# The first products of two feed-forwards, taken with 512 moving columns instead of 256

## The chip, the cores and the metric

One core of one Trainium2 chip. The metric is the device time of one execution of the whole program in microseconds (us), lower is better. Times are medians of several executions.

## What is computed

A transformer block (recurrent unit beside latent attention, cross attention to a memory, feed-forward) and a second one (dilated and differential attention, feed-forward, gated linear attention, eight experts), for 256 tokens of width 1024, all in 32-bit floats. The change touches the first half of the two feed-forwards alone:

```python
# first block: D_FF = 2816, w_up is 1024 x 5632
gu = rms_norm(x, ffn_norm) @ w_up
gu = depthwise_conv(gu, ffn_conv_w, ffn_conv_b, 1, 1)     # 3 taps over the tokens, per column
g, u = gu[..., :D_FF], gu[..., D_FF:]
x = x + (jax.nn.silu(g) * u) @ w_down

# second block: the same without the convolution
h = rms_norm_2(x, ffn_norm_2)
x = x + (jax.nn.silu(h @ w_gate) * (h @ w_up)) @ w_down
```

## The kernel before

**Numbers in two parts.** TensorE multiplies 32-bit numbers in a form (fp32r) that holds fewer bits. So each operand is kept as a rounded part and the rest, and a product is the sum of three: rounded x rounded, rounded x rest, rest x rounded. `wh` and `wl` are the two parts of the weights, `hTh` and `hTl` those of the 256 normalised tokens (features on the partitions, tokens along the row, 8 tiles `k` of 128 features).

**Weights as a stream.** All weights lie in HBM as 458 units of 128 x 2048 numbers (1 MB). SyncE loads them one after another into 7 buffers `raw`, each as soon as VectorE is through with the unit 7 before it. ScalarE rounds each unit into one of 3 buffers `wh` (`hi_to`, L1444 to L1451, instruction L1450), as soon as the product that used the buffer before is done. VectorE subtracts and gets the rest into `wl` (`lo_to`, L2203 to L2209, instruction L2207). `hi_to(m)` and `lo_to(m)` stand in the programs of the two engines where the author put them, and each engine does its instructions strictly in order.

**A feed-forward.** 22 rounds `f`, one unit each: 128 columns of the gate and 128 of the up projection (`i` = 0 and 1). In `gated` (L819) TensorE makes both with `feature_major` (L549), through `split_product` (L419): for each of 8 `k` a matmul of the rounded weights with 256 columns of rounded tokens (L424) and one with 256 columns of rests (L428), both adding into the same 256 columns of PSUM, then 8 matmuls of the rests of the weights with the rounded tokens (L435). So a round has 48 matmuls of 256 moving columns. The rounds go through PSUM banks 0 to 3, gate and up side by side in one bank; a round waits for the read of the one four before (`gated_read`).

In the first feed-forward ScalarE then forms the middle tap and bias out of PSUM (L1750, two instructions of 256 columns) and rounds the unit three rounds ahead (L1450); VectorE forms the rest of that unit (L2207), adds the two outer taps out of PSUM (L2635, four instructions of 255 columns, with a wait on its own result after the second), and for the round before it does sigmoid x gate (L2644) and x up (L2645), and for the round before that the rest of the hidden value (L2623). ScalarE does the sigmoid (L1757) and the rounding of the hidden value (L1761). In the second feed-forward there is no convolution: VectorE multiplies bank `f % 4` with the row of token scales (L2860, 512 columns) into `gu2`, and then come sigmoid (L1904), L2865, L2866, L2207, L2623.

`project_out` (L533) then multiplies the 22 hidden tiles with the second weights: 11 units, 24 matmuls of 512 columns each, into banks 4 to 7.

Of the kernel before, what the change touches and what calls it, by code (L numbers as in the profile page):

```python
# [26 lines left out]
P = 128  # L27
# [80 lines left out]
def build(nc, units_d, consts_d, cols_d, rows_d, lru_w_d, x_d, mem_d, pos_d, out_d):  # L108
# [8 lines left out]
    hT_at = nc.sbuf_base  # L117
    hTh = sb("hTh", [KD, S], F32R)
    hTl = sb("hTl", [KD, S], F32R)
    xn = sb("xn", [TT, D])  # L120
# [43 lines left out]
    def row(name, n):  # L164
# [18 lines left out]
        "gu": dict(ffn=FT, ffn2=FT), "in_copied": dict(lru=8, mem=6), "in_read": dict(attn=12, hgrn=14),  # L183
        "gated": dict(lru=1, hgrn=2), "product": dict(lru=2, ffn=FT, ffn2=FT),
        "in": dict(lru=8, mem=8, attn=16, hgrn=24), "gated_sigmoid": dict(ffn=FT, ffn2=FT), "gated_read": dict(ffn=FT, ffn2=FT),
# [65 lines left out]
    cv = [[xn[:, b // 2, 512 * (b % 2) + 256 * i:512 * (b % 2) + 256 * (i + 1)] for i in range(2)] for b in range(4)]  # L251
    sg = [area(12288 + 256 * b, S) for b in range(4)]
    gu2 = [xn[:, b // 2, 512 * (b % 2):512 * (b % 2 + 1)].rearrange("p (i s) -> p i s", i=2) for b in range(4)]

# [149 lines left out]
    def _(pe):  # L404
# [144 lines left out]
        def feature_major(out, w, c):  # L549
# [3 lines left out]
                                 ready=tile_ready, weights="stationary")  # L553

        def token_major(name, n0, srch, srcl, banks, width=HALF):

            for half in range(2):
                w = by_k(unit(n0 + half), KD // 2, width)
                for t in range(TT):
                    ts = slice(t * P, (t + 1) * P)  # L560
                    ks = [4 * half + k for k in range(4)]
                    ins = split_product(ps[:, banks[t], 0:width],
                                        [(srch[:, k, ts], srcl[:, k, ts], w[0][:, k - 4 * half, :], w[1][:, k - 4 * half, :])
                                         for k in ks], first=(half == 0), last=(half == 1),
                                        ready=lambda j: tile_ready(4 * half + j))
                    if half == 1 or t == 1:
                        counted(ins, name)
                release(n0 + half, name)
# [249 lines left out]

        def gated(stage, n0):  # L819
            for f in range(FT):  # L820
                w = by_k(unit(n0 + f), KD, S)
                if f >= 4:
                    pe.wait_ge(*reached(stage + "_gated_read", f - 3))
                for i in range(2):
                    ins = feature_major(ps[:, f % 4, i * S:(i + 1) * S], w, i)
                counted(ins, stage + "_gu")
                release(n0 + f, stage + "_gu")
                if f == 0 and stage == "ffn2":
                    pe.wait_ge(*reached("scale_diag", 1))
                    counted(accumulate(ps[:, 4, 0:S], [(ones, scale_diag.rearrange("p t c -> p (t c)"))]), "scale_ps")  # L830

        norm("ffn_norm")
        gated("ffn", UNITS_AT["w_up"])
        project_out("ffn_x_change", UNITS_AT["w_down"], FT, hidh, hidl, lambda k: pe.wait_ge(*reached("ffn_hid", k + 1)))

# [216 lines left out]
        norm("ffn_norm_2")  # L1052
        gated("ffn2", UNITS_AT["ffn_gate_up"])
        project_out("ffn2_x_change", UNITS_AT["ffn_w_down"], FT, hidh, hidl,
# [385 lines left out]
    def _(act):  # L1440
# [302 lines left out]
        for f in range(FT + 2):  # L1743
            if f < FT:
                act.wait_ge(*reached("ffn_gu", f + 1))
                if f >= 4:
                    act.wait_ge(*reached("ffn_product", f - 3))
                for i in range(2):
                    c = f + i * FT
                    ins = A(cv[f % 4][i], ps[:, f % 4, i * S:(i + 1) * S], ACT.Identity,  # L1750
                            scale=col("ffn_conv_w", 2 * FT + c), bias=col("ffn_conv_b", c))
                ins.then_inc(sem("ffn_centre"), 1)
                hi_to(UNITS_AT["w_up"] + f + 4)
            if 1 <= f <= FT:
# [144 lines left out]
        scales(1)  # L1899
        for f in range(FT + 2):  # L1900
            hi_to(UNITS_AT["ffn_gate_up"] + f + 4)
            if f < FT:
# [284 lines left out]
    def _(dve):  # L2187
# [438 lines left out]
        for f in range(FT + 2):  # L2626
            if f < FT:
                dve.wait_ge(*reached("ffn_centre", f + 1))
                lo_to(UNITS_AT["w_up"] + f + 4)
                for tap in range(2):  # L2630
                    for i in range(2):
                        w = col("ffn_conv_w", tap * 2 * 2 * FT + f + i * FT)
                        y, src = cv[f % 4][i], ps[:, f % 4, i * S:(i + 1) * S]
                        a, b = (slice(1, S), slice(0, S - 1)) if tap == 0 else (slice(0, S - 1), slice(1, S))
# [222 lines left out]
        for f in range(FT + 2):  # L2857
            if f < FT:
                dve.wait_ge(*reached("ffn2_gu", f + 1))
                V.tensor_tensor(gu2[f % 4], ps[:, f % 4, :].rearrange("p (i s) -> p i s", i=2), both,  # L2860
                                ALU.mult).then_inc(sem("ffn2_gated_read"), 1)
            if 1 <= f <= FT:
# [508 lines left out]
```

## Time and profile before

| | |
|---|---|
| median of 3 executions | 1872.81 us (1871.18 to 1873.44) |
| the profiled execution, its own time | 1872.04 us |
| its span, first to last instruction | 1870.2 us |
| TensorE busy | 1824.6 us, 98% |
| VectorE busy | 1477.8 us, 79% |
| ScalarE busy | 1232.8 us, 66% |
| mean granted TensorE clock | 0.994 |
| moved from and to HBM | 492 MB, mean 263 GB/s |

The profile calls TensorE PE (its weight loads PEld), VectorE DVE, ScalarE ACT. Busy time of TensorE is no measure of its pace, since its matmuls overlap: one of 256 columns is shown as 284 ns long while they start every 120 ns. The pace is read from the distance of starts. In a row of the view in order of time the first number is the start, the second the duration, both in us; where a row merges several instructions (x4), the duration is that of all.

### The profile page before, as it was taken

The page shows a single profiled execution, that of the slowest core. Times are in us where ns is not written, and L with a number is a line of the kernel's source. Part 1 is how long each engine was busy: PE and PEld are TensorE (multiplying, and loading weights), DVE is VectorE, ACT ScalarE, POOL GpSimd, SP SyncE. Part 2 cuts the span into 40 slices and gives each one's busy share as a digit, 9 for nine tenths or more (in the row PEclk, how much of TensorE's full clock was granted, in tenths as well). Part 3 has the DMA queues.
Part 4 walks back from the last instruction along what each step waited for, and adds up shares of the span by engine and source line. Part 5 has one row for each costly group of instructions (what it writes and reads, how often), then busy time and mean ns, then how long its engine had stood idle before and what let it go on. Part 6 is the DMA issues. An engine that isn't in the chain of part 4 may idle for free.

```text
span 1870.2 us, 25929 instructions
## 1 busy us (share of the span) xinstructions
PE 1824.6 (98%) x9976; PEld 1558.8 (83%) x9976; DVE 1477.8 (79%) x1502; ACT 1232.8 (66%) x1292; POOL 25.5 (1%) x27
## 2 busy tenths in 40 slices
PE   9989999999899999999999999999999999999998
PEld 7867899887789998987788888888888888888886
DVE  7975688657667765675988988889889899898886
ACT  6966556455654434663777777777777777777775
POOL 0000000000000000000000000000000000000000
PEclk9999999999999999999999999999999999999999
DMA  9422445543235554534699999999999999999994
GB/s 356 158 86 90 158 180 181 202 174 117 73 115 189 187 184 144 185 125 146 229 381 358 391 373 358 375 364 391 376 343 378 374 391 367 341 391 372 379 378 162
DMA packets 69091, 491.97 MB, mean 263 GB/s; under 512 B 7792, under 2 KB 8176, under 8 KB 10096
## 3 DMA queue, kind: packets, MB, share of 16 engines
q1 hardware_dynamic: 67248, 484.33, 68.0%
q0 software_dynamic: 1728, 6.03, 1.6%
q8 instruction: 81, 1.33, 0.3%
q14 instruction: 34, 0.28, 0.0%
HBM read 485.09 MB, written 5.24 MB: 262 GB/s over the span
## 4 chain that ended last, share of the span: by engine, by line
PE 86%; DVE 7%; ACT 5%; issue 2%; POOL 0%; DVEq 0%; ACTq 0%; POOLq 0%
PE ps L424 26%; PE ps L433 20%; PE ps L426 20%; PE ps L435 5%; PE ps L428 5%; DVE wl L2207 2%; PE ps L1370 1%; ACT wh L1450 1%; PE ps L444 1%; PE ps L1271 1%; PE ps L584 1%; DVE hTl L2265 1%; ACT hTh L1488 1%; PE ps L854 1%; PE ps L855 1%
## 5 line engine op out<-in xcount | busy, mean ns | idle before, releaser
L3163 DVE TENSOR_TENSOR wl<-raw,wh 128x2048 fp32r<-128x2048 f32 x334 | 761.2, 2291 | 88.1 <-ACT wh L2089 87.4
L2089 ACT ACTIVATE wh<-raw 128x2048 fp32r<-128x2048 f32 x333 | 637.9, 1918 | 182.5 <-PE ps L433 182.5
L424 PE MATMUL ps<-wh,hTh 128*128 128x512 f32 (+2 forms) x1128 | 443.0, 394 | 5.5 <-DVE hTl L2538 1.5
L426 PE MATMUL ps<-wh,hTl 128*128 128x512 f32 (+2 forms) x1128 | 434.7, 386 | 0.0
L2207 DVE TENSOR_TENSOR wl<-raw,wh 128x2048 fp32r<-128x2048 f32 x124 | 283.6, 2290 | 123.8 <-ACT wh L1450 123.4
L1450 ACT ACTIVATE wh<-raw 128x2048 fp32r<-128x2048 f32 x125 | 238.6, 1914 | 138.0 <-PE ps L433 70.2
L433 PE MATMUL ps<-wl,hTh 128*128 128x512 f32 (+2 forms) x1128 | 300.9, 386 | 0.0
L424 PE MATMUL ps<-wh,work_r 128*128 128x512 f32 x648 | 254.8, 393 | 0.0
L424 PEld LDWEIGHTS ps<-wh,hTh 128*128 128x128 f32 x1128 | 212.0, 188 | 48.8 <-issue 4.2
L426 PE MATMUL ps<-wh,work_r 128*128 128x512 f32 x648 | 252.5, 390 | 0.0
L426 PEld LDWEIGHTS ps<-wh,hTl 128*128 128x128 f32 x1128 | 212.2, 188 | 40.1
L433 PEld LDWEIGHTS ps<-wl,hTh 128*128 128x128 f32 x1128 | 209.8, 188 | 42.9
L424 PE MATMUL ps<-hTh,wh 128*128 128x256 f32 x896 | 223.5, 286 | 4.3 <-DVE hTl L2265 4.0
L428 PE MATMUL ps<-hTl,wh 128*128 128x256 f32 x896 | 221.4, 284 | 0.0
L433 PE MATMUL ps<-wl,work_r 128*128 128x512 f32 x648 | 200.3, 390 | 0.5 <-DVE wl L3163 0.5
L424 PEld LDWEIGHTS ps<-hTh,wh 128*128 128x128 f32 x896 | 171.7, 192 | 7.5 <-issue 5.0
L428 PEld LDWEIGHTS ps<-hTl,wh 128*128 128x128 f32 x896 | 171.8, 192 | 0.1
L433 PEld LDWEIGHTS ps<-wl,work_r 128*128 128x128 f32 x648 | 121.2, 188 | 28.1 <-DVE wl L3163 2.8
L424 PEld LDWEIGHTS ps<-wh,work_r 128*128 128x128 f32 x648 | 121.7, 188 | 25.7 <-issue 1.0
L426 PEld LDWEIGHTS ps<-wh,work_r 128*128 128x128 f32 x648 | 121.7, 188 | 24.5
L435 PE MATMUL ps<-hTh,wl 128*128 128x256 f32 x896 | 126.3, 284 | 0.0
L435 PEld LDWEIGHTS ps<-hTh,wl 128*128 128x128 f32 x896 | 116.1, 192 | 0.0
(442 smaller groups left out, 1548.9 us busy)
## 6 DMA issues: line engine op xcount, KB each, us to landing
raw<-in_units SPq DMA_DIRECT2D x458, 1024.0 KB, 6.8
x<-in_x SPq DMA_DIRECT2D x2, 512.0 KB, 5.9
work<-in_lru_w SPq DMA_DIRECT2D x1, 1024.0 KB, 16.0
xn<-in_mem SPq DMA_DIRECT2D x1, 1024.0 KB, 14.2
out<-x POOLq DMA_DIRECT2D x2, 512.0 KB, 6.4
consts<-in_consts POOLq DMA_DIRECT2D x1, 768.0 KB, 4.5
consts<-in_consts SPq DMA_DIRECT2D x1, 356.0 KB, 12.5
cols<-in_cols SPq DMA_DIRECT2D x1, 202.0 KB, 2.6
```

What stands on the lines that cost most here:

```text
L424: nc.tensor.matmul(out, sh, mh, start=(first and j == 0), stop=False)
L426: nc.tensor.matmul(out, sl, mh, start=False, stop=False)
L428: nc.tensor.matmul(out, sh, ml, start=False, stop=False)
L433: ins = nc.tensor.matmul(out, sh, ml, start=False, stop=done)
L435: ins = nc.tensor.matmul(out, sl, mh, start=False, stop=done)
L444: ins = nc.tensor.matmul(out, l, r, start=(first and j == 0), stop=(last and j == len(pairs) - 1))
L584: nc.tensor.matmul(ps[:, 7, :], junk[:, 0:P], junk[:, 0:HALF], start=True, stop=True)
L854: nc.tensor.matmul(out, hTh[:, k, ts], hi[:, o], start=first, stop=False, skip_group_check=u == 2)
L1450: A(wh[:, n % SPLIT, :], raw[:, n % RAW, :], ACT.Copy).then_inc(sem("hi_made"), 1)
L2089: A(wh[:, n % SPLIT, :], raw[:, n % RAW, :], ACT.Copy).then_inc(sem("hi_made"), 1)
L2207: V.tensor_tensor(wl[:, n % SPLIT, :], raw[:, n % RAW, :], wh[:, n % SPLIT, :].bitcast(F32), ALU.subtract).then_inc(sem("lo_made"), 1)
L3163: V.tensor_tensor(wl[:, n % SPLIT, :], raw[:, n % RAW, :], wh[:, n % SPLIT, :].bitcast(F32), ALU.subtract).then_inc(sem("lo_made"), 1)
```

## The change

`hTh` and `hTl` become the two halves of one buffer `hT_both` at the same place. In the new `halves_beside` one matmul per `k` takes the rounded tokens and the rests, 512 moving columns, against the rounded weights, and writes 512 columns of PSUM: the first 256 hold rounded x rounded, the others rounded x rest. The 8 matmuls of the weights' rests add into the first 256 as before. Gate and up now have a bank each, so a round fills two banks and every second round uses the same ones. What the matmuls no longer add has to be added afterwards: ScalarE copies the first halves (2 x 256 columns) out of PSUM into SBUF, VectorE adds the second halves (2 x 256 columns, read from PSUM). In the first feed-forward middle tap and outer taps then read that sum from SBUF; in the second, the sum is multiplied with the scales in SBUF. TensorE waits for the sum of the round two before (`summed`) in place of the read of the one four before. In the first feed-forward ScalarE rounds the next weights ahead of the middle tap instead of behind it, and VectorE waits for `ffn_centre` behind the weights' rest instead of ahead of it.

```diff
-    hTh = sb("hTh", [KD, S], F32R)
-    hTl = sb("hTl", [KD, S], F32R)
+    hT_both = sb("hT_both", [2, KD, S], F32R)
+    hTh, hTl = hT_both[:, 0, :, :], hT_both[:, 1, :, :]
...
+    gu = [area(11264 + 512 * b, 2, S) for b in range(2)]
...
+        def halves_beside(out, w, c):
+
+            cs = slice(c * P, (c + 1) * P)
+            for k in range(KD):
+                tile_ready(k)
+                nc.tensor.matmul(out, w[0][:, k, cs], hT_both[:, :, k, :], start=(k == 0), stop=False)
+            rest_made()
+            for k in range(KD):
+                ins = nc.tensor.matmul(out[:, 0:S], w[1][:, k, cs], hTh[:, k, :], start=False, stop=(k == KD - 1))
+            return ins
...
-        def gated(stage, n0):
+        def gated_beside(stage, n0):
             for f in range(FT):
                 w = by_k(unit(n0 + f), KD, S)
-                if f >= 4:
-                    pe.wait_ge(*reached(stage + "_gated_read", f - 3))
+                if f >= 2:
+                    pe.wait_ge(*reached(stage + "_summed", f - 1))
                 for i in range(2):
-                    ins = feature_major(ps[:, f % 4, i * S:(i + 1) * S], w, i)
+                    ins = halves_beside(ps[:, 2 * (f % 2) + i, :], w, i)
...
@@ ScalarE, first feed-forward
                 act.wait_ge(*reached("ffn_gu", f + 1))
+                b = 2 * (f % 2)
+                A(gu[f % 2], ps[:, b:b + 2, 0:S], ACT.Copy).then_inc(sem("ffn_first"), 1)
+                hi_to(UNITS_AT["w_up"] + f + 4)
                 if f >= 4:
                     act.wait_ge(*reached("ffn_product", f - 3))
+                act.wait_ge(*reached("ffn_summed", f + 1))
                 for i in range(2):
                     c = f + i * FT
-                    ins = A(cv[f % 4][i], ps[:, f % 4, i * S:(i + 1) * S], ACT.Identity,
+                    ins = A(cv[f % 4][i], gu[f % 2][:, i, :], ACT.Identity,
                             scale=col("ffn_conv_w", 2 * FT + c), bias=col("ffn_conv_b", c))
                 ins.then_inc(sem("ffn_centre"), 1)
-                hi_to(UNITS_AT["w_up"] + f + 4)
@@ ScalarE, second feed-forward
+            if f < FT:
+                b = 2 * (f % 2)
+                act.wait_ge(*reached("ffn2_gu", f + 1))
+                A(gu2[f % 4], ps[:, b:b + 2, 0:S], ACT.Copy).then_inc(sem("ffn2_first"), 1)
             hi_to(UNITS_AT["ffn_gate_up"] + f + 4)
@@ VectorE, first feed-forward
+                b = 2 * (f % 2)
+                dve.wait_ge(*reached("ffn_first", f + 1))
+                V.tensor_tensor(gu[f % 2], ps[:, b:b + 2, S:2 * S], gu[f % 2], ALU.add).then_inc(sem("ffn_summed"), 1)
+                lo_to(UNITS_AT["w_up"] + f + 4)
+                dve.wait_ge(*reached("ffn_summed", f + 1))
                 dve.wait_ge(*reached("ffn_centre", f + 1))
-                lo_to(UNITS_AT["w_up"] + f + 4)
...
-                        y, src = cv[f % 4][i], ps[:, f % 4, i * S:(i + 1) * S]
+                        y, src = cv[f % 4][i], gu[f % 2][:, i, :]
@@ VectorE, second feed-forward
                 dve.wait_ge(*reached("ffn2_gu", f + 1))
-                V.tensor_tensor(gu2[f % 4], ps[:, f % 4, :].rearrange("p (i s) -> p i s", i=2), both,
-                                ALU.mult).then_inc(sem("ffn2_gated_read"), 1)
+                b = 2 * (f % 2)
+                dve.wait_ge(*reached("ffn2_first", f + 1))
+                V.tensor_tensor(gu2[f % 4], ps[:, b:b + 2, S:2 * S], gu2[f % 4], ALU.add).then_inc(sem("ffn2_summed"), 1)
+                dve.wait_ge(*reached("ffn2_summed", f + 1))
+                V.tensor_tensor(gu2[f % 4], gu2[f % 4], both, ALU.mult).then_inc(sem("ffn2_gated_read"), 1)
```

In the order of the instructions this is a round of the first feed-forward on VectorE, before (L2207 makes the weights' rest, L2635 are the outer taps, L2644 and L2645 the products, L2623 the hidden value's rest; in brackets what an instruction waits for):

```order
L2207 TENSOR_TENSOR wl<-raw,wh 128x2048 [waits hi_made,ffn_centre]
L2635 SCALAR_TENSOR_TENSOR xn<-ps,cols,xn 128x255 x2
L2635 SCALAR_TENSOR_TENSOR xn<-ps,cols,xn 128x255 [waits vector_step]
L2635 SCALAR_TENSOR_TENSOR xn<-ps,cols,xn 128x255
L2644 TENSOR_TENSOR work<-work,xn 128x256 [waits gated_read,gated_sigmoid]
L2645 TENSOR_TENSOR work<-work,xn 128x256 [waits vector_step]
L2623 TENSOR_TENSOR work_r<-work,work_r 128x256 [waits hid_hi]
```

and now, with the new line numbers (L2649 is the sum of the halves, L2226 the weights' rest, L2658 the outer taps):

```order
L2649 TENSOR_TENSOR work<-ps,work 128x512 [waits first]
L2226 TENSOR_TENSOR wl<-raw,wh 128x2048 [waits hi_made]
L2658 SCALAR_TENSOR_TENSOR xn<-work,cols,xn 128x255 [waits ffn_centre,summed]
L2658 SCALAR_TENSOR_TENSOR xn<-work,cols,xn 128x255
L2658 SCALAR_TENSOR_TENSOR xn<-work,cols,xn 128x255 [waits vector_step]
L2658 SCALAR_TENSOR_TENSOR xn<-work,cols,xn 128x255
L2667 TENSOR_TENSOR work<-work,xn 128x256 [waits gated_read,gated_sigmoid]
L2668 TENSOR_TENSOR work<-work,xn 128x256 [waits vector_step]
L2642 TENSOR_TENSOR work_r<-work,work_r 128x256 [waits hid_hi]
```

The sum stands ahead of the weights' rest, which no longer waits for ScalarE's middle tap. On TensorE a round of the first feed-forward is now this (L561 with both kinds of columns, L564 the weights' rests; there are two such pairs of lines to a round):

```order
L561 MATMUL ps<-hT_both,wh 128x512 [waits summed,hi_made]
L561 MATMUL ps<-hT_both,wh 128x512 x7
L564 MATMUL ps<-hT_both,wl 128x256 [waits lo_made]
L564 MATMUL ps<-hT_both,wl 128x256 x7
L561 MATMUL ps<-hT_both,wh 128x512 x8
L564 MATMUL ps<-hT_both,wl 128x256 [waits lo_made]
L564 MATMUL ps<-hT_both,wl 128x256 x7
```

That is 16 matmuls of 512 columns and 16 of 256 in place of 48 of 256.

## Rows read from the trace of the kernel before

**Rows 1.** The page: busy time by engine, and the DMA engines in 40 slices.
```profile
PE 1824.6 (98%) x9976; PEld 1558.8 (83%) x9976; DVE 1477.8 (79%) x1502; ACT 1232.8 (66%) x1292; POOL 25.5 (1%) x27
...
DMA  9422445543235554534699999999999999999994
```

**Rows 2.** By stretch: us; busy (x) of PE, PEld, DVE, ACT, POOL; PEclk, DMA share, GB/s.
```profile
203.30:208.40 5.10, 5.09 (x24) 5.10 (x25) 5.10 (x8) 2.94 (x5) 0.00 (x0) 0.52 0.00 0
208.40:332.30 123.90, 123.90 (x1035) 123.90 (x1034) 103.68 (x160) 72.59 (x103) 0.00 (x0) 1.00 0.53 187
547.00:675.00 128.00, 127.89 (x1058) 127.26 (x1059) 91.55 (x113) 59.69 (x74) 0.00 (x0) 1.00 0.50 182
1000.00:1860.00 860.00, 859.46 (x3941) 711.73 (x3941) 758.82 (x458) 640.11 (x447) 19.31 (x15) 1.00 0.95 365
```

**Rows 3.** TensorE in order of time, first feed-forward, 24 matmuls (half a round) apart.
```profile
263.12 0.28 PE L424 MATMUL ps<-hTh,wh 128*128 128x256 f32 x1
...
265.04 1.12 PE L435 MATMUL ps<-hTh,wl 128*128 128x256 f32 x8
266.00 0.28 PE L424 MATMUL ps<-hTh,wh 128*128 128x256 f32 x1
```

**Rows 4.** TensorE in order of time, 512-column matmuls of a product going out.
```profile
349.95 0.39 PE L424 MATMUL ps<-wh,work_r 128*128 128x512 f32 x1
...
352.67 0.39 PE L424 MATMUL ps<-wh,work_r 128*128 128x512 f32 x1
```

**Rows 5.** TensorE in order of time, attention input: 512 columns behind 256.
```profile
411.08 1.12 PE L859 MATMUL ps<-wl,hTh 128*128 128x256 f32 x8
412.04 0.40 PE L854 MATMUL ps<-wh,hTh 128*128 128x512 f32 x1
...
413.88 1.07 PE L859 MATMUL ps<-wl,hTh 128*128 128x512 f32 x4
```

**Rows 6.** VectorE in order of time, first feed-forward, one round and the next start.
```profile
260.49 2.29 DVE L2207 TENSOR_TENSOR wl<-raw,wh 128x2048 fp32r<-128x2048 f32 x1 [0.65 <-ACT wh L1450]
262.70 1.78 DVE L2635 SCALAR_TENSOR_TENSOR xn<-ps,cols,xn 128x255 f32<-128x255 f32 x4
264.39 0.42 DVE L2644 TENSOR_TENSOR work<-work,xn 128x256 f32<-128x256 f32 x1
264.84 0.42 DVE L2645 TENSOR_TENSOR work<-work,xn 128x256 f32<-128x256 f32 x1
265.19 0.42 DVE L2623 TENSOR_TENSOR work_r<-work,work_r 128x256 fp32r<-128x256 f32 x1
266.25 2.29 DVE L2207 TENSOR_TENSOR wl<-raw,wh 128x2048 fp32r<-128x2048 f32 x1 [0.64 <-ACT wh L1450]
```

**Rows 7.** ScalarE in order of time, the same round of the first feed-forward.
```profile
257.56 1.02 ACT L1750 ACTIVATE xn<-ps,cols 128x256 f32<-128x256 f32 x2 [2.33 <-PE ps L435]
258.47 1.91 ACT L1450 ACTIVATE wh<-raw 128x2048 fp32r<-128x2048 f32 x1
260.28 0.41 ACT L1757 ACTIVATE work<-xn 128x256 f32<-128x256 f32 x1
260.58 0.41 ACT L1761 ACTIVATE work_r<-work 128x256 fp32r<-128x256 f32 x1
```

**Rows 8.** VectorE, second feed-forward, in order of time.
```profile
565.83 0.69 DVE L2860 TENSOR_TENSOR xn<-ps,junk 128x512 f32<-128x512 f32 x1 [1.46 <-PE ps L435]
566.44 0.42 DVE L2865 TENSOR_TENSOR work<-work,xn 128x256 f32<-128x256 f32 x1
...
567.84 2.29 DVE L2207 TENSOR_TENSOR wl<-raw,wh 128x2048 fp32r<-128x2048 f32 x1 [0.53 <-ACT wh L1450]
```

**Rows 9.** Groups of instructions by line and form: those nearest to the new ones.
```profile
L1933 ACT ACTIVATE work<-ps 128x512 f32<-128x512 f32 x4 | 2.3, 585 | 0.0
L2394 DVE SCALAR_TENSOR_TENSOR work<-work,cols 128x256 f32<-128x256 f32 x24 | 10.0, 480 | 0.3
L2573 DVE TENSOR_TENSOR work<-work 128x512 f32<-128x512 f32 x2 | 1.4, 692 | 0.4 <-ACT work L1689 0.4
```

More of the change, by code:

```diff
@@ L183, in build @@
         "gu": dict(ffn=FT, ffn2=FT), "in_copied": dict(lru=8, mem=6), "in_read": dict(attn=12, hgrn=14),
-        "gated": dict(lru=1, hgrn=2), "product": dict(lru=2, ffn=FT, ffn2=FT),
+        "first": dict(ffn=FT, ffn2=FT), "summed": dict(ffn=FT, ffn2=FT), "gated": dict(lru=1, hgrn=2), "product": dict(lru=2, ffn=FT, ffn2=FT),
         "in": dict(lru=8, mem=8, attn=16, hgrn=24), "gated_sigmoid": dict(ffn=FT, ffn2=FT), "gated_read": dict(ffn=FT, ffn2=FT),
@@ L832, in _ @@
         norm("ffn_norm")
-        gated("ffn", UNITS_AT["w_up"])
+        gated_beside("ffn", UNITS_AT["w_up"])
         project_out("ffn_x_change", UNITS_AT["w_down"], FT, hidh, hidl, lambda k: pe.wait_ge(*reached("ffn_hid", k + 1)))
@@ L1052, in _ @@
         norm("ffn_norm_2")
-        gated("ffn2", UNITS_AT["ffn_gate_up"])
+        gated_beside("ffn2", UNITS_AT["ffn_gate_up"])
         project_out("ffn2_x_change", UNITS_AT["ffn_w_down"], FT, hidh, hidl,
```

## Prediction

> **What bounds the kernel now.** I read the page first. TensorE is busy 98% of the span, VectorE 79%, ScalarE 66% [rows 1]. A busy TensorE says little about its pace, so I went to the stretches. The first feed-forward's 22 rounds run from 203.3 to 332.3 us, the second's from 547 to 675 us; in both TensorE is covered from end to end, and the DMA engines are about half busy (0.53 and 0.50) [rows 2]. So neither stage waits for weights, and whatever shortens TensorE's work there shortens the kernel, as long as the other engines keep up. The DMA line climbs to 9 tenths only in the second half [rows 1], in the experts (0.95 over 860 us) [rows 2]. That does not swallow a gain: SyncE's loads are released by VectorE's use of older units, not by the clock, so if a feed-forward ends earlier, every later load moves with it.
>
> The pace of TensorE is read from starts. In the feed-forward 24 matmuls of 256 columns take 263.12 to 266.00 = 2.88 us, 120 ns each [rows 3]; a round is 48 of them, 5.76 us. A product of 512 columns starts every 226.7 ns (12 in 2.72 us) [rows 4]. At the granted clock of 1.00, the level of 2.4 GHz [rows 2], the columns alone are 106.7 and 213.3 ns, so both sizes carry the same 13.3 ns on top. That is what the change goes for: the columns stay the same (48 x 256 = 16 x 512 + 16 x 256), the instructions fall from 48 to 32.
>
> **TensorE's new round.** By the two paces alone a half round is 8 x 226.7 + 8 x 120 = 2.77 us instead of 2.88. But the program has a place with just the new pattern: in the attention's input a run of 8 matmuls of 512 columns stands right behind 256-column ones, and it takes 412.04 to 413.88 = 1.84 us, 230 ns each, 0.03 more than 8 x 226.7 [rows 5]. The 8 ahead of it take 0.96 us (411.08 to 412.04), the 120 ns of always. I take this row, since the new kernel goes from 256 to 512 columns in every half round: 1.84 + 0.96 = 2.80 us, 0.08 less than now, 5.60 us a round. Of 2 x 44 = 88 half rounds two are left out: the first of the first stage runs at a granted clock of 0.52, nearly all at the 1.2 GHz level [rows 2], where fewer instructions showed me no saving, and the first of the second waits for its inputs tile by tile. 86 x 0.08 = **6.9 us saved**. The upper end is 0.107 (226.7 ns from the first matmul on), 9.2 us. The lower end is nothing: no row has a moving operand in two pieces 8 KB apart, and were the 13.3 ns paid per 256 columns of a piece, 512 would cost 240. I stay near the upper end because a contiguous 512 is the nearest row.
>
> The Trainium skill ("TensorE: Matmul & The Clock Gate", section Back-to-back issue gap) gives N / 2.4 + 2.5 ns as the gap of isolated warm matmuls, that is 2.5 ns an instruction. By that rule the 86 x 8 = 688 removed instructions would be worth 1.7 us. The rows above show 13.3, so here trace and rule differ.
>
> **VectorE in the first feed-forward.** This is the tight place. A round by starts: rest of the weights 2.21 (260.49 to 262.70), four outer taps 1.69, the two products 0.45 and 0.35, the hidden rest another 0.35 taken from the like-sized one before it: 5.05 us, then 0.64 us idle until ScalarE's `wh` [rows 6]. Added is a sum of 512 columns; the nearest row is the 512-column product with one operand in PSUM, 0.69 us long, with the next instruction 0.61 us behind it [rows 8]. New round: 5.66 us, against 5.60 of TensorE. At the other end, if the next one waits for its full length and a semaphore (0.75), 5.80; if it overlapped wholly, 5.05. That the taps now read SBUF changes nothing: 480 ns for a 256-column one from SBUF [rows 9], four of 255 from PSUM in 1.78 us [rows 6].
>
> VectorE being 0.06 slower does not stall TensorE at once, because there is slack. A fresh round would go: ScalarE's copy ends 0.65 us after TensorE's round (585 ns [rows 9]), the sum ends at 1.3, but `wh` is ready only at 2.6 (1.91 us behind the copy [rows 7]); then 5.05 more, so the next sum starts at 7.65, that is 2.05 us after the end of TensorE's next round. From there on `wh` is ready in time and the lag grows by 0.06 a round. TensorE needs the sum of round f when it begins round f+2, 5.60 us after the end of round f: the lag may be 5.60 - 0.75 = 4.85. Slack 2.8 us, growth over 18 rounds 1.1: **no stall, 0 us**. At 5.80 the growth is 3.6, a stall of 0.8. Behind the 22nd round VectorE drains its lag under the outgoing product, whose first three units have their parts made by then; the fourth is needed 16.3 us (3 x 24 x 226.7 ns) after the stage ends, its rest 0.9 later, and lag, sum, weights, taps, two rounds' products, hidden rounding and the two parts of that unit add up to about 14.4 (3.2 + 0.6 + 2.2 + 1.7 + 2.0 + 0.5 + 1.9 + 2.3).
>
> **ScalarE, first stage.** Round by starts: middle tap 0.91, rounding of weights 1.81, sigmoid 0.30, hidden rounding 0.41 at most [rows 7], plus the copy 0.59: 4.0 of 5.60 us. It now waits for the sum too, but everything it owes VectorE comes at most 2 us after that sum, while VectorE has 2.21 us of weights to do: 0 us.
>
> **Second stage.** VectorE idles 1.46 + 0.53 = 2.0 us a round [rows 8]. Added: the sum in its full length, since its own result is awaited, 0.75; the product with the scales stays at 0.69 out of SBUF (692 ns for such a one) [rows 9]. 1.25 us of idle become what is left, less 0.16 of shorter round. TensorE's new wait, for the sum of two rounds ago, is met about 1.4 us after that round: 0 us. ScalarE has room.
>
> **Sum.** -6.9 us. The profiled execution's own time is 1872.04 us, 1.8 above its span; it becomes 1865.1. The median of the runs is 0.8 above that execution, so the forecast for the median is 1872.8 - 6.9 = **1865.9 us**, -0.37%. Runs differ by about 0.1%, and 0.2% (3.7 us) is about what a measurement of this kernel can tell from no change; faster means below 1869.1.
>
> **Rivals.**
> (a) *The full saving.* Runs of 512 start at 226.7 ns at once: -9.2, 1863.6 us. For it: most 512-column rows. Against: the one run behind 256 columns.
> (b) *VectorE binds the first stage mildly.* The stall is 18 x (round - 5.60) - 2.8 us. For a round of 5.90, 2.6 us, 1868.5; of 6.14, 6.9 us, 1872.8. For it: only 0.06 us is missing already, and semaphore waits have been added. Against: the parts of the round are read from starts, and the sum has a row close to it.
> (c) *Instructions are not what costs.* The two-piece operand takes 240 ns: no gain, 1872.8 us. By the skill's 2.5 ns it would be 1871.1. For it: no row shows two pieces. Against: the same 13.3 ns at both sizes.
> (d) *Slower: VectorE's round above 6.14 us*, from where the loss in the first stage exceeds the whole saving. Its place would be the wait for `wh` (1.3 us in a fresh round, above) coming back in every round instead of once: because ScalarE's copy and rounding now stand behind its own wait for the sum of the round before. The round would be 5.66 + 1.3 = 6.96, the stall 18 x 1.36 - 2.8 = 21.7, the time 1887.6 us. From the sum's end ScalarE needs 0.91 + 0.30 + 0.41 + 0.59 + 1.91, with waits 4.4 us, and VectorE comes to that point 5.66 us later; it decides if that path grows by over 1.2 us. Nothing in the rows does that.
>
> **How the numbers follow.** Forecast (1864.8 to 1867.0) 0.63, (a) 0.14, (b) 0.10, (c) 0.06, (d) 0.07. Faster: 0.63 + 0.14 + half of (b) = 0.82; same: the other half and (c) = 0.11; slower 0.07. The range 1863.0 to 1868.9 holds the forecast, (a) and the milder half of (b), 0.82.
>
> **What would show it.** Right: starts of the 512-column matmuls in the stages 227 to 233 ns apart, rounds of 5.60 us (5.55 for (a)) in both stages, VectorE without idle time from the third round on in the first stage, and TensorE without a wait for `summed`; the experts as long as before, only earlier. Wrong: 240 ns starts (c); TensorE waiting for VectorE's sum late in the first stage (b) or in every round (d); the second stage gaining no 3.4 us while the first does, or something behind the stages growing by what they saved.

## The result, and the profile after

| | before | changed |
|---|---|---|
| median of 5 executions each | 1871.51 us (1871.18 to 1873.44) | 1862.87 us (1861.71 to 1864.01) |
| ratio | | 0.9948, 95% interval 0.9937 to 0.9959 |
| profiled execution, own time | 1872.04 | 1861.83 |
| its span | 1870.2 | 1859.7 |
| instructions of TensorE (matmuls) | 9976 | 9272 |

The change made the kernel 8.6 us faster (by the interval of the ratio 7.7 to 11.8). The forecast was 6.9 us and 1865.9 us, and the measured time lies 0.1 us below the lower end of the range. The page of the changed kernel, busy time by engine and the DMA engines in 40 slices:

```profile
PE 1815.2 (98%) x9272; PEld 1518.8 (82%) x9272; DVE 1502.6 (81%) x1546; ACT 1260.7 (68%) x1336; POOL 25.5 (1%) x27
...
DMA  9422455543235554444699999999999999999994
```

TensorE has 704 matmuls fewer, VectorE and ScalarE have 44 instructions more each, and the picture is otherwise that of [rows 1]. By stretch, with the stages' new bounds (us; busy time and count of PE, PEld, DVE, ACT, POOL; granted clock, DMA share, GB/s):

```profile
202.49:327.20 124.71, 124.71 (x705) 109.18 (x705) 119.45 (x186) 89.42 (x129) 0.00 (x0) 0.99 0.51 186
390.26:536.69 146.43, 138.68 (x777) 113.20 (x777) 98.08 (x180) 88.23 (x167) 0.00 (x0) 0.98 0.32 113
539.87:664.18 124.31, 124.21 (x707) 108.38 (x707) 104.17 (x134) 72.05 (x95) 0.00 (x0) 1.00 0.52 187
664.18:1859.50 1195.32, 1180.04 (x5762) 981.29 (x5760) 993.12 (x727) 835.38 (x649) 24.06 (x21) 1.00 0.84 320
```

The first stage took 128.9 us before (203.3 to 332.2) and 124.7 now, the second 128.1 and 124.3: 4.2 and 3.8 us less. All that lies behind the second stage takes 1195.5 us (the last row stops 0.2 us short of the end), against 1195.2 from the same point before: what the stages save reaches the end. TensorE in order of time, first stage:

```profile
257.37 2.00 PE L561 MATMUL ps<-hT_both,wh 128*128 128x512 f32 x8
259.21 1.11 PE L564 MATMUL ps<-hT_both,wl 128*128 128x256 f32 x8
260.16 2.00 PE L561 MATMUL ps<-hT_both,wh 128*128 128x512 f32 x8
262.00 1.12 PE L564 MATMUL ps<-hT_both,wl 128*128 128x256 f32 x8
262.95 2.00 PE L561 MATMUL ps<-hT_both,wh 128*128 128x512 f32 x8
```

Eight matmuls of 512 columns take 1.84 us from start to start (257.37 to 259.21), just as in [rows 5], the eight of 256 behind them 0.95. A half round is 2.79 us, in place of 2.88 [rows 3]. VectorE, one round of the first stage:

```profile
256.91 0.68 DVE L2649 TENSOR_TENSOR work<-ps,work 128x512 f32<-128x512 f32 x1
257.51 2.28 DVE L2226 TENSOR_TENSOR wl<-raw,wh 128x2048 fp32r<-128x2048 f32 x1
259.71 1.79 DVE L2658 SCALAR_TENSOR_TENSOR xn<-work,cols,xn 128x255 f32<-128x255 f32 x4
261.41 0.42 DVE L2667 TENSOR_TENSOR work<-work,xn 128x256 f32<-128x256 f32 x1
261.87 0.43 DVE L2668 TENSOR_TENSOR work<-work,xn 128x256 f32<-128x256 f32 x1
262.21 0.42 DVE L2642 TENSOR_TENSOR work_r<-work,work_r 128x256 fp32r<-128x256 f32 x1
262.54 0.68 DVE L2649 TENSOR_TENSOR work<-ps,work 128x512 f32<-128x512 f32 x1
```

Where [rows 6] had 0.64 us of idle there is none: the round is 262.54 - 256.91 = 5.63 us, and it is longer than TensorE's 5.59. Who waited for whom in the first stage (us in total, times, longest):

```profile
ACT work L1759 <- PE ps L564: 23.2, 22, 4.7
ACT xn L1766 <- DVE work L2649: 13.4, 19, 1.2
DVE wl L2226 <- ACT wh L1462: 3.7, 4, 1.4
```

ScalarE waits for VectorE's sum in 19 rounds, up to 1.2 us; VectorE waited for `wh` in its first rounds only (1.1, 1.0 and 0.2 us; the fourth wait of the row, 1.4 us, lies behind the stage); no wait of TensorE for the sum is in the list, in this stage or in the second.

**Where the rest of the difference lies.** The two profiled spans differ by 10.5 us, 8.0 of it in the stages. The kernel starts its first product 0.9 us earlier, and the attention between the stages took 148.5 us before, 2.1 more than now, with the same instructions:

```profile
395.31:543.83 148.52, 139.89 (x776) 114.89 (x777) 98.35 (x180) 88.15 (x167) 0.00 (x0) 0.97 0.31 111
```

That row is of the kernel before; its granted clock is 0.97, that of the changed kernel there 0.98. The experiments show whether this belongs to the change.

### The profile page after: what moved, and what is told of

The parts are those of the page before. It is cut to its first block, busy times and chain, and to the rows that moved or that the text cites. A ratio compares the mean times of both kernels' runs of the same rounds, so it can differ in the third digit from the quotient of the medians.

```text
span 1859.7 us, 24634 instructions
## 1 busy us (share of the span) xinstructions
PE 1815.2 (98%) x9272; PEld 1518.8 (82%) x9272; DVE 1502.6 (81%) x1546; ACT 1260.7 (68%) x1336; POOL 25.5 (1%) x27
## 3 DMA queue, kind: packets, MB, share of 16 engines
q8 instruction: 76, 1.25, 0.3%
## 4 chain that ended last, share of the span: by engine, by line
PE 85%; DVE 7%; ACT 5%; issue 2%; POOL 0%; DVEq 0%; ACTq 0%; POOLq 0%
PE ps L425 21%; PE ps L434 20%; PE ps L427 20%; PE ps L561 9%; PE ps L564 5%; DVE wl L2226 2%; ACT wh L1462 1%; PE ps L1382 1%; PE ps L445 1%; PE ps L1283 1%; PE ps L436 1%; PE ps L429 1%; PE ps L596 1%; ACT hT_both L1500 1%; DVE hT_both L2284 1%
## 5 line engine op out<-in xcount | busy, mean ns | idle before, releaser
L425 PE MATMUL ps<-wh,hT_both 128*128 128x512 f32 (+2 forms) x1128 | 443.0, 394 | 5.5 <-DVE hT_both L2557 1.5
L427 PE MATMUL ps<-wh,hT_both 128*128 128x512 f32 (+2 forms) x1128 | 434.7, 386 | 0.0
L2226 DVE TENSOR_TENSOR wl<-raw,wh 128x2048 fp32r<-128x2048 f32 x124 | 283.2, 2288 | 94.0 <-ACT wh L1462 93.7
L434 PE MATMUL ps<-wl,hT_both 128*128 128x512 f32 (+2 forms) x1128 | 300.9, 386 | 0.0
L425 PEld LDWEIGHTS ps<-wh,hT_both 128*128 128x128 f32 x1128 | 212.0, 188 | 48.8 <-issue 4.2
L427 PEld LDWEIGHTS ps<-wh,hT_both 128*128 128x128 f32 x1128 | 212.2, 188 | 40.2
L434 PEld LDWEIGHTS ps<-wl,hT_both 128*128 128x128 f32 x1128 | 209.9, 188 | 42.9
L561 PE MATMUL ps<-hT_both,wh 128*128 128x512 f32 x704 | 179.0, 395 | 2.7 <-DVE hT_both L2284 2.5
L561 PEld LDWEIGHTS ps<-hT_both,wh 128*128 128x128 f32 x704 | 127.0, 190 | 27.5 <-issue 3.0
L564 PEld LDWEIGHTS ps<-hT_both,wl 128*128 128x128 f32 x704 | 96.4, 191 | 7.0
L564 PE MATMUL ps<-hT_both,wl 128*128 128x256 f32 x704 | 98.4, 283 | 0.0
L2118 ACT ACTIVATE work<-ps 128x512 f32<-128x512 f32 x56 | 33.5, 599 | 40.7 <-PE ps L434 40.7
L425 PE MATMUL ps<-hT_both,wh 128*128 128x256 f32 x192 | 48.6, 290 | 2.1 <-DVE hT_both L2284 2.0
```

Of the source, the lines that this page charges most:

```text
L425: nc.tensor.matmul(out, sh, mh, start=(first and j == 0), stop=False)
L427: nc.tensor.matmul(out, sl, mh, start=False, stop=False)
L434: ins = nc.tensor.matmul(out, sh, ml, start=False, stop=done)
L561: nc.tensor.matmul(out, w[0][:, k, cs], hT_both[:, :, k, :], start=(k == 0), stop=False)
L564: ins = nc.tensor.matmul(out[:, 0:S], w[1][:, k, cs], hTh[:, k, :], start=False, stop=(k == KD - 1))
L2118: A(esg, ps[:, 2 * (c % 2), :], ACT.Silu).then_inc(sem("gate_silu"), 1)
```

## The experiments

Two theories of what pays: the number of TensorE's instructions (each removed one is worth a fixed time), or what came with it (banks, order on ScalarE and VectorE). And two on VectorE: its round of 5.63 us binds, or slack covers it. Stage times below run from the first matmul of a stage to the first of the outgoing product.

| kernel | first stage | between | second stage | behind | span |
|---|---|---|---|---|---|
| before | 128.9 | 214.8 | 128.1 | 1195.2 | 1870.2 |
| changed | 124.7 | 212.7 | 124.3 | 1195.5 | 1859.7 |
| first stage only | 124.6 | 212.7 | 128.1 | 1196.9 | 1864.8 |
| second stage only | 128.7 | 212.6 | 124.3 | 1197.0 | 1865.9 |
| two of 256 for each 512 | 128.9 | 213.2 | 128.1 | 1196.7 | 1870.3 |
| 16 of 512, then 16 of 256 | 124.9 | 213.2 | 123.9 | 1195.5 | 1860.7 |
| one piece of 512 | 125.4 | 213.2 | 124.6 | 1196.5 | 1863.0 |
| one VectorE instruction more | 128.5 | 213.9 | 124.3 | 1195.5 | 1864.5 |
| two more | 134.6 | 215.6 | 125.7 | 1195.4 | 1873.7 |
| old order on ScalarE and VectorE | 183.8 | 221.0 | 125.6 | 1195.4 | 1929.1 |
| changed, once more | 125.0 | 213.3 | 124.3 | 1196.9 | 1862.7 |
| 16 of 512, then 16 of 256, once more | 124.5 | 213.2 | 123.9 | 1195.3 | 1858.5 |

**One stage at a time.** In `e1_first_only` the second stage has the old `gated`, copy and sum removed there:

```diff
-        gated_beside("ffn2", UNITS_AT["ffn_gate_up"])
+        gated("ffn2", UNITS_AT["ffn_gate_up"])
```

> Only the first feed-forward is changed, the second is as before. Theory A (each matmul removed is worth a fixed part of some 11 ns, 0.087 us a half round): 3.8 us in the rounds of the first stage, plus about 0.5 us in its first half round if the clock rises as early as in the changed kernel; so 3.8 to 4.5 us faster than before, half rounds of 2.79 us in the first stage and 2.88 in the second. Theory B (VectorE, at 5.64 us a round, takes part of it back in the first stage): TensorE waits for the sum of the halves, gain under 3 us. Theory C (part of the 8.6 us is the clock in other stages, not the change): the profile shows other stages differing by more than 1 us where the granted clock differs.

Measured: 1867.06 against 1872.79 us, ratio 0.9972 (0.9963 to 0.9982). `e2_second_only` has the old code in the first stage:

```diff
-        gated_beside("ffn", UNITS_AT["w_up"])
+        gated("ffn", UNITS_AT["w_up"])
```

> Only the second feed-forward is changed. Theory A: 43 half rounds x 0.087 = 3.7 us faster than before. Together with the first stage alone this should give 7.5 to 8.2 us; what the changed kernel gained beyond that would be the clock in other stages or the measurement (theory C).

Measured: 1868.11 against 1872.79 us, ratio 0.9975 (0.9966 to 0.9984). By medians the gains are 5.7 and 4.7 us, together 10.4, both above what was expected (3.8 to 4.5, and 3.7) and together above the 8.6 of the whole change. By stage times they are 4.3 and 3.7, together 8.0, as expected. The changed stage has the same length whether or not the other is changed (124.6 and 124.7; 124.3 and 124.3), so by the stages the two gains add, and VectorE takes nothing back in the first (theory B falls). The stretches between and behind differ by up to 2 us among kernels that are the same there. Behind the second stage there is a pattern. Seven of the twelve profiles have 1195.2 to 1195.5 us there, five have 1196.5 to 1197.0. In these five, and in no other, the granted clock from 725 to 750 us is 0.93 in place of 1.00. The changed kernel stands on both sides. The first row is its second profile, the other its first one:

```profile
731.00:741.00 10.00, 9.37 (x61) 8.95 (x62) 8.35 (x14) 7.03 (x14) 0.00 (x0) 0.83 0.38 141
731.00:741.00 10.00, 9.91 (x81) 9.51 (x80) 8.50 (x10) 7.15 (x12) 0.00 (x0) 1.00 0.56 204
```

So theory C holds for that stretch: its 1 to 2 us go with the clock, whichever kernel it is.

**Is it the number of instructions?** Everything of the change stays, only the 512 columns are written as twice 256:

```diff
-                nc.tensor.matmul(out, w[0][:, k, cs], hT_both[:, :, k, :], start=(k == 0), stop=False)
+                nc.tensor.matmul(out[:, 0:S], w[0][:, k, cs], hTh[:, k, :], start=(k == 0), stop=False, skip_group_check=True)
+                nc.tensor.matmul(out[:, S:2 * S], w[0][:, k, cs], hTl[:, k, :], start=False, stop=(k == KD - 1), skip_group_check=True)
             rest_made()
             for k in range(KD):
-                ins = nc.tensor.matmul(out[:, 0:S], w[1][:, k, cs], hTh[:, k, :], start=False, stop=(k == KD - 1))
+                ins = nc.tensor.matmul(out[:, 0:S], w[1][:, k, cs], hTh[:, k, :], start=False, stop=(k == KD - 1), skip_group_check=True)
```

> Everything as in the changed kernel (banks, copy, sum, order on ScalarE and VectorE), but each 512-column matmul is written as two of 256 into the two halves of the bank, 48 matmuls a round again. Theory A: half rounds back at 2.88 us, time within 1.5 us of before. Theory D (the gain comes from the new order on the other engines or the banks, not from the number of instructions): it stays near the changed kernel, 7 to 9 us faster than before. VectorE has 0.12 us idle a round in the first stage, so no stall is expected.

Measured: 1873.38 us, ratio 1.0002 (0.9993 to 1.0011). TensorE, the starts of two half rounds:

```profile
257.83 0.28 PE L562 MATMUL ps<-hT_both,wh 128*128 128x256 f32 x1
...
259.39 1.12 PE L565 MATMUL ps<-hT_both,wl 128*128 128x256 f32 x8
260.36 0.28 PE L561 MATMUL ps<-hT_both,wh 128*128 128x256 f32 x1
...
262.27 1.12 PE L565 MATMUL ps<-hT_both,wl 128*128 128x256 f32 x8
263.24 0.28 PE L561 MATMUL ps<-hT_both,wh 128*128 128x256 f32 x1
```

260.36 to 263.24 is 2.88 us again, and both stages are back at 128.9 and 128.1. So the gain in the stages comes from the 704 joined pairs; banks, copy, sum and order together are worth nothing there and cost nothing (theory D falls). Copy and sum, 88 instructions, are fully hidden. One thing this run does not separate: each matmul has a weight load of its own, and with 9976 matmuls in place of 9272 it has as many more weight loads, although the two halves use the same weights. Whether the saved time belongs to the matmul or to its weight load is not shown; below, "instruction" means the two together.

**What a change from 256 to 512 columns costs.** All 16 matmuls of 512 columns of a round first, then all 16 of 256:

```diff
+            for c in range(2):
+                cs = slice(c * P, (c + 1) * P)
+                for k in range(KD):
+                    tile_ready(k)
+                    nc.tensor.matmul(outs[c], w[0][:, k, cs], hT_both[:, :, k, :], start=(k == 0), stop=False)
             rest_made()
...
+            for c in range(2):
+                cs = slice(c * P, (c + 1) * P)
+                for k in range(KD):
+                    ins = nc.tensor.matmul(outs[c][:, 0:S], w[1][:, k, cs], hTh[:, k, :], start=False, stop=(k == KD - 1))
```

> In each round all 16 matmuls of 512 columns come first, then all 16 of 256: one change from 256 to 512 a round in place of two. Theory A with a price for each such change (0.03 us, 8 matmuls of 512 in 1.84 instead of 1.81 us): a round of 5.56 instead of 5.59 us, 44 x 0.03 = 1.3 us faster than the changed kernel, if VectorE's 5.64 us a round in the first stage lets it; there the growth of its lag is 0.08 a round, 1.5 us over 18 rounds, inside the slack of 2.8, so still no stall. Rival (every run of 512 columns is slower by 3 ns a matmul in this stage, wherever it begins): a round stays at 5.59, same time as the changed kernel.

Measured: 1862.53 us, 0.3 us below the changed kernel's median where 1.3 was expected, ratio 0.9941 (0.9928 to 0.9955). TensorE, second stage:

```profile
603.95 3.82 PE L562 MATMUL ps<-hT_both,wh 128*128 128x512 f32 x16
607.60 2.08 PE L567 MATMUL ps<-hT_both,wl 128*128 128x256 f32 x16
609.52 3.82 PE L562 MATMUL ps<-hT_both,wh 128*128 128x512 f32 x16
```

Sixteen of 512 take 3.65 us, that is 0.03 more than 16 x 226.7 ns = 3.627, where two runs of eight take 3.68. A round is 5.57 us, and the second stage 0.4 us shorter (22 x 0.02). The starts in the trace say where the extra time sits. Averaged over the first stage behind its first round, the distances behind the first five matmuls of a run of 512 are 233, 236, 228, 232 and 231 ns, and from the sixth on 226.7, in the changed kernel's runs of 8 and in these of 16 alike: 0.028 us a run. Part of it comes back: the first matmul of 256 behind a run of 512 has the next one 113 ns behind it and the second 119, where the others have 120. So a pair of changes, 256 to 512 and back, costs 0.020 us, and a run of 16 saves one such pair a round.

**One piece or two.** The moving 512 columns are one run of 2 KB; this sums rounded tokens of two tiles, and leaves the rests of the tokens out:

```diff
-                tile_ready(k)
-                nc.tensor.matmul(out, w[0][:, k, cs], hT_both[:, :, k, :], start=(k == 0), stop=False)
+                tile_ready(min(k + 1, KD - 1))
+                j = min(k, KD - 2)
+                nc.tensor.matmul(out, w[0][:, k, cs], hTh[:, j:j + 2, :].rearrange("p k s -> p (k s)"), start=(k == 0), stop=False)
```

> The 512 moving columns lie in one piece of 2 KB (rounded tokens of tiles k and k+1) in place of two pieces 8 KB apart; the rests of the tokens are left out and other products are summed, so only the time counts. Theory A: a run of 8 still takes 1.84 us behind 256-column matmuls, time as the changed kernel within 1 us. Rival (the two pieces cost the extra 3 ns a matmul): runs of 8 in 1.81 us, 88 x 0.03 = 2.6 us faster than the changed kernel.

Measured: 1865.22 us, ratio 0.9964 (0.9953 to 0.9976). TensorE, first stage:

```profile
256.02 2.00 PE L562 MATMUL ps<-hT_both,wh 128*128 128x512 f32 x8
257.86 1.12 PE L565 MATMUL ps<-hT_both,wl 128*128 128x256 f32 x8
258.81 2.00 PE L562 MATMUL ps<-hT_both,wh 128*128 128x512 f32 x8
```

1.84 and 2.79 us, to the hundredth those of the changed kernel: the gap of 8 KB costs nothing. Its time is 2.3 us above the changed kernel's 1862.87 (1.25 above the 1863.97 of its second series), more than the 1 us I expected. Its stages are 0.7 and 0.3 us longer: in the first half round of each it waits for one tile more than the changed kernel. Behind the stages it is one of the five profiles with the lower clock at 725 to 750 us, 1.0 us longer than the changed kernel's first.

**How near VectorE is to the limit.** One and two more instructions in each round of the first stage:

```diff
                 ins.then_inc(sem("ffn_gated_read"), 1)
+                V.tensor_tensor(junk[:, 0:256], consts[:, 0:S], consts[:, 0:S], ALU.mult)
```

> One more VectorE instruction of 256 columns (SBUF, result unused, 0.34 us from start to start) in every round of the first feed-forward, behind the outer taps. Theory of the slack: round of VectorE 5.64 + 0.34 = 5.98 us against 5.59 of TensorE; its lag grows by 0.39 a round, reaches the allowed 4.85 us after about 7 rounds, and TensorE then waits 18 x 0.39 - 2.8 = 4.3 us in all: about 1867.5 us. Rival (no slack: every round is the longer of the two, 22 x 0.39 = 8.6 us, some 1871.5). Rival (VectorE is not near any limit): as the changed kernel.

> Two such instructions. Round of VectorE 6.32, growth 0.73 a round, stall 18 x 0.73 - 2.8 = 10.4 us, so about 1873.5 us, the gain of the change gone and a little more. Against one extra instruction the step should be 18 x 0.34 = 6.1 us, since the slack is spent already.

Measured: 1868.75 us, ratio 0.9985 (0.9975 to 0.9995), and 1875.75 us, ratio 1.0018 (1.0009 to 1.0028). The medians lie 1.25 and 2.25 us above the expected 1867.5 and 1873.5. The first stage, which the theory is about, takes 3.8 and 9.9 us more than in the changed kernel, expected 4.3 and 10.4, and the step between them is 6.1, as expected; the rest lies outside that stage or in the scatter of the executions. The slack is real: without it one instruction would have cost 8.6 us. Its size came out a little larger than reckoned: with one more instruction VectorE's lag grows by 0.38 us a round and stops growing at 5.1 us, in the eleventh round, not at 4.85 after about seven. With two, TensorE waits in each of the last 14 rounds (two of them; the idle time before, and what ended it, in brackets):

```profile
293.57 2.08 PE L561 MATMUL ps<-hT_both,wh 128*128 128x512 f32 x8 [0.47 <-DVE work L2649]
...
299.88 2.06 PE L561 MATMUL ps<-hT_both,wh 128*128 128x512 f32 x8 [0.48 <-DVE work L2649]
```

299.88 - 293.57 = 6.31 us is VectorE's round.

**The order on ScalarE and VectorE.** As the changed kernel, but with the two engines' old order:

```diff
@@ ScalarE
-                hi_to(UNITS_AT["w_up"] + f + 4)
                 if f >= 4:
                     act.wait_ge(*reached("ffn_product", f - 3))
...
                 ins.then_inc(sem("ffn_centre"), 1)
+                hi_to(UNITS_AT["w_up"] + f + 4)
@@ VectorE
-                lo_to(UNITS_AT["w_up"] + f + 4)
                 dve.wait_ge(*reached("ffn_summed", f + 1))
                 dve.wait_ge(*reached("ffn_centre", f + 1))
+                lo_to(UNITS_AT["w_up"] + f + 4)
```

> As the changed kernel, but in the first feed-forward ScalarE forms the middle tap ahead of the rounding of the next weights, and VectorE waits for the middle tap ahead of the weights' rest, as before the change. Then sum, middle tap and rounding stand in a row in each round: VectorE idles from the end of its sum for 0.92 + 1.85 + 0.1 = 2.9 us, its round is 0.75 + 2.9 + 5.0 = 8.6 us, less what it could do meanwhile (nothing, its order is fixed). Stall 18 x 3.0 - 2.8 = 51 us: about 1914 us. This is rival (d) of the prediction made true. If instead the order does not matter, the time is the changed kernel's.

Measured: 1930.15 us, ratio 1.0307 (1.0290 to 1.0325). VectorE's round, then ScalarE's, then TensorE:

```profile
254.05 0.68 DVE L2649 TENSOR_TENSOR work<-ps,work 128x512 f32<-128x512 f32 x1
257.85 2.29 DVE L2226 TENSOR_TENSOR wl<-raw,wh 128x2048 fp32r<-128x2048 f32 x1 [3.12 <-ACT wh L1462]
...
262.89 0.68 DVE L2649 TENSOR_TENSOR work<-ps,work 128x512 f32<-128x512 f32 x1
```

```profile
254.83 1.09 ACT L1765 ACTIVATE xn<-work,cols 128x256 f32<-128x256 f32 x2 [4.85 <-DVE work L2649]
255.83 1.89 ACT L1462 ACTIVATE wh<-raw 128x2048 fp32r<-128x2048 f32 x1
```

```profile
254.88 3.65 PE L561 MATMUL ps<-hT_both,wh 128*128 128x512 f32 x8 [3.02 <-DVE work L2649]
258.36 1.11 PE L564 MATMUL ps<-hT_both,wl 128*128 128x256 f32 x8
```

VectorE idles 3.1 us in every round, which from the fifth on is 262.89 - 254.05 = 8.84 us long, and TensorE waits for the sum. Expected 8.6 and 1914 us; it is 16 us worse. The first stage is 59.1 us longer than in the changed kernel, 8 more than the 51 expected, of which the longer round explains 18 x 0.24 = 4 us. The other 8 us lie between the stages (221.0 us against 212.7), where the program is the same. The clock goes with this: between the stages its mean is 0.96 against 0.98, and in the first stage (203.2 to 387.0 us) it is 0.90 against 0.99. The run of eight behind the wait of 3.02 us takes 3.48 us in place of 1.84, near the 3.41 us of 8 x 512 columns at the 1.2 GHz level:

```profile
203.20:387.00 183.80, 143.37 (x704) 121.71 (x705) 118.58 (x185) 83.94 (x124) 0.00 (x0) 0.90 0.35 123
```

So the two lines that the change moves, and that look like a detail in the diff, are worth 67 us between the two kernels, 59 of them in the stage itself.

**Changed kernel and runs of 16 side by side.** Neither kernel has a new edit.

> The changed kernel once more, on the same chip and against the same runs of before as the next one. The stages alone give 7.5 us (86 half rounds x 0.087) and 0.5 us more where the first half round meets the higher clock; with the single stages' 5.7 and 4.7 us as measured it would be up to 10.4. Theory of the clock (a time moves by a microsecond or two with where the low-clock windows fall outside the changed stages): the gain lies between 8 and 10 us and the runs with a higher mean clock are the shorter ones.

> The order with 16 matmuls of 512 and then 16 of 256 a round once more, beside the changed kernel. Rounds of 5.57 in place of 5.59 us in both stages: 44 x 0.023 = 1.0 us faster than the changed kernel, which is less than the spread of single runs; likely the medians differ by 0 to 2 us in its favour.

Measured against the same executions of before (1872.39 us): the changed kernel 1863.97 us, ratio 0.9950 (0.9936 to 0.9963); runs of 16 1861.24 us, ratio 0.9943 (0.9930 to 0.9957). In both series runs of 16 has the lower median (by 0.3 and 2.7 us), and its rounds are shorter by 0.02 us, but the intervals overlap widely: 1 us is what the rounds show, and the times cannot tell it. In the repeated profile of the changed kernel the stages took 125.0 and 124.3 us, together 7.6 less than before, and the span was 1862.7, 7.5 less. There the other stretches cancel. The gain of 8.4 us lies in the expected 8 to 10. That executions with a higher mean granted clock are shorter holds only in part. In the first series of the changed kernel it does: two at 0.994 have spans below 1859.8, the one at 0.992 has 1861.9. In the second the shortest, 1858.9, has 0.994, but the longest, 1862.7, has 0.993, and three at 0.992 have 1861.8 to 1861.9.

## Why the prediction was wrong by a little

The mechanism was right: fewer instructions on TensorE, no wait of TensorE for VectorE, and the end of the kernel moving along. The size was short, and the range was cut too close.

- **TensorE's round, the step that failed.** The term "1.84 + 0.96 = 2.80 us, 0.08 less than now" was mis-sized: the half round is 1.84 + 0.95 = 2.79 us, 0.087 less. The run of eight with 512 columns came out as taken from [rows 5]. The 0.96 is what was wrong, "the 120 ns of always". In [rows 5] the eight of 256 columns stand behind other matmuls of 256 columns, the last of these being

```profile
410.96 0.28 PE L855 MATMUL ps<-wh,hTl 128*128 128x256 f32 x1
```

In the new round they stand behind matmuls of 512 columns, and the first two then take 113 and 119 ns in place of 120. So my row priced the change from 256 to 512 columns (0.028 us) and not the change back, which gives 0.008 us. The trace of before had that one too, where 256 columns follow 512:

```profile
406.29 0.28 PE L854 MATMUL ps<-wh,hTh 128*128 128x256 f32 x1
406.40 0.28 PE L855 MATMUL ps<-wh,hTl 128*128 128x256 f32 x1
406.52 0.28 PE L854 MATMUL ps<-wh,hTh 128*128 128x256 f32 x1
```

Over 86 half rounds 0.087 makes 7.5 us, not 6.9, and the second profile of the changed kernel shows it (stages 7.6 us less than before with 0.2 in the first half round, span 7.5 less).
- **The first half round, left out at nothing.** It took 4.60 us (202.49 to 207.09) in place of 5.10 [rows 2], and the mean granted clock in it was 0.63 in place of 0.52: it began at the higher level, fell and rose again. In the second profile of the same kernel it took 4.94 (203.17 to 208.11) at 0.54. So this is 0.2 to 0.5 us that goes with the clock and differs from execution to execution; the removed instructions have no part in it that these profiles show.
- **The lower end of the range.** I put it 0.6 us below rival (a). What the sum left out on the fast side (0.5 us here, up to 2 us in the attention between, 0.9 at the start) is no effect of the removed instructions. Their scatter is in every median: those of before lay between 1871.51 and 1872.79 over four series, and the forecast was counted from 1872.81. The changed kernel's own two medians are 1862.87 and 1863.97; the second lies inside the range, so which side of the end a series falls on is in part luck. The too small 6.9 us is not.
- **Rival (a)**, 9.2 us, is nearer to the measured 8.6 than the forecast but has the wrong reason: no run of 512 in the stages has 226.7 ns from its first matmul on. It adds 9.2 us in the rounds, and the rounds give 7.5.
- **What stays open.** By medians the change is worth 8.6 and 8.4 us in the two series, and the stages alone 5.7 and 4.7; by the rounds it is 7.5, with the first half round up to 8.0, and 4.3 and 3.7. So 0.4 to 1.4 us of each gain by medians is not in the stages. The kernel with all of the change but the 512 columns does not show it (1873.38 against 1872.79 us, with an interval of 1.7 us to either side). A granted clock that is low less often when the stages are shorter would fit: its mean over all executions is 0.9918 before (57 of them), 0.9916 with two of 256, 0.9929 in the changed kernel (10) and 0.9936 with runs of 16 (10), and 0.001 of 1870 us is 1.9 us of full clock (an estimate). But the kernel with one piece of 512, its stages nearly as short, has 0.9920, and no run sets the clock by itself. So the cause is not shown.
- **VectorE in the first stage.** Round 5.66 predicted, 5.63 measured; lag 2.05 predicted at its start and 2.1 measured from the fourth round on; lag at the last round 3.2 predicted, 330.18 - 327.20 = 3.0 measured; stall none. Both kernels with more VectorE work follow the formula of the slack within 0.5 us in the stage. (b) did not happen, but one instruction of 0.34 us a round would have made it happen.
- **ScalarE.** "0 us" held; its wait for the sum, up to 1.2 us a round, is idle time that nobody waits for.
- **Second stage.** "0 us" held too. VectorE has 0.83 us idle before each sum, where 1.25 - 0.16 = 1.09 was reckoned, and TensorE has no wait for it.
- **Rival (c)** fell: two pieces cost nothing, and a run of eight took 1.84 us, 230 ns each, not 240. The 688 instructions fewer in 86 half rounds gave 7.5 us, 10.8 ns each; that is 13.3 ns each less the 0.020 us that the changes between 512 and 256 columns cost in each half round. The 2.5 ns that the Trainium skill ("TensorE: Matmul & The Clock Gate", Back-to-back issue gap) gives for isolated warm matmuls is not what an instruction costs in this stream of 32-bit matmuls with a new weight load each.
- **Rival (d)** did not happen. A wait for `wh` in every round can be had, though: with the old order it came in every round and made the first stage 59 us longer. It is not quite the chain that (d) describes, since there the middle tap and the weights' rest stood in the new order; (d) was priced at 21.7 us for 1.3 us a round, and the old order has 3.1 us a round and a lower clock besides.
- **The end.** Work behind the second stage took as long as before, 1195.5 against 1195.2 us and within 2 us in every kernel, so the gain was not swallowed by the DMA-heavy second half.

## What to carry to other kernels

Where TensorE is covered from end to end, count its instructions (a matmul and its weight load) and not only its columns: products that share their stationary operand are worth joining up to the full 512 columns, if an add outside is cheaper than what it saves and has a place to hide. That place has to be checked on the engine that is nearly full: its round may exceed TensorE's a little for a limited number of rounds, and the allowance is the slack that the buffers give. And where a new wait is put into two engines that feed each other, put what the next round needs (here the weights' rounding) ahead of it: here the order of two lines was worth over seven times the change.

## What the runs showed of the hardware that I had not expected

A run of 512-column matmuls behind 256-column ones starts slower: 233, 236, 228, 232 and 231 ns behind its first five, then 226.7, so 0.028 us in all, whether the run is 8 long (1.84 us) or 16 long (3.65), and whether the moving operand is one piece or two. The first two of 256 columns behind a run of 512 are quicker than the later ones, 113 and 119 ns against 120. What causes either is not shown.

And the same program took different times outside the stages: behind the second stage 1195.2 to 1195.5 us, or 1196.5 to 1197.0 where the granted clock was low for a while near 735 us. The stretch between the stages took 212.6 to 214.8 us where the first stage was not held up by VectorE for long, and 215.6 and 221.0, with a mean granted clock of 0.97 and 0.96, in the two kernels where TensorE had waited in most rounds before. Comparisons under 2 us need the rounds themselves, not the total.
